# RG-LRU gates as four 64x64 products on quarters of the array, in a two-layer hybrid decoder trunk

## What is computed

```
def rglru_branch(xb, conv_w, conv_b, wa, ba, wx, bx, lam):
    xc = causal_dwconv(xb, conv_w) + conv_b
    xh = xc.reshape(Bsz, S, LRU_HEADS, LRU_HEAD_DIM)          # 8 heads of 64 channels
    r = sigmoid(einsum('bshi,hij->bshj', xh, wa) + ba)        # gate a
    ig = sigmoid(einsum('bshi,hij->bshj', xh, wx) + bx)       # gate x
    log_a = -LRU_C * r * softplus(-lam)
    a = exp(log_a);  mult = sqrt(-expm1(2.0 * log_a))
    h = scan(a, mult * ig * xc)
```

## Time and profile before

| | us |
|---|---|
| median of three runs (1820.25 to 1823.0) | 1821.43 |
| profiled execution, its time | 1824.21 |
| profiled execution, its span | 1822.4 |
| PE busy (share of the span) | 1668.1 (92%) |
| DVE busy | 1252.0 (69%) |
| ACT busy | 772.3 (42%) |
| POOL busy | 232.8 (13%) |
| mean DMA rate over the span | 206 GB/s |

### The profile page before, as it was taken

How to read it: one execution, slowest core, us unless ns; L and a number is a source line. 1 busy time by engine, 2 the same in 40 slices (tenths; PEclk the granted TensorE clock), 3 DMA queues, 4 the chain that set the end, 5 groups by cost and what they waited for, 6 DMA issues and landing times.

```text
span 1822.4 us, 23064 instructions
## 1 busy us (share of the span) xinstructions
PE 1668.1 (92%) x7527; PEld 1295.7 (71%) x7527; DVE 1252.0 (69%) x2361; ACT 772.3 (42%) x1014; POOL 232.8 (13%) x281
## 2 busy tenths in 40 slices
PE   2339999989999999999998999999999999999995
PEld 1237778767777877777886777777877777776884
DVE  5885984796598479666862587398468558743758
ACT  2135444554444454432126554554555464442220
POOL 2142111111111111100004111111111111100000
PEclk9559999999999999999998999999999999999998
DMA  7999888988987998867646888987888887755422
GB/s 261 379 330 255 199 209 212 234 218 200 232 209 205 215 234 208 209 199 273 206 142 180 196 192 193 216 191 192 205 196 202 189 204 186 178 163 200 146 93 104
DMA packets 322945, 376.07 MB, mean 206 GB/s; under 512 B 27064, under 2 KB 224032, under 8 KB 319784
## 3 DMA queue, kind: packets, MB, share of 16 engines
q1 hardware_dynamic: 294632, 272.36, 46.4%
q0 software_dynamic: 28224, 102.77, 31.3%
HBM read 261.81 MB, written 10.51 MB: 149 GB/s over the span
## 4 chain that ended last, share of the span: by engine, by line
PE 58%; DVE 29%; issue 6%; DMA 3%; ACT 2%; SPq 1%; DVEq 0%; POOL 0%; ACTq 0%; POOLq 0%
PE bank L1012 18%; PE bank L975 11%; PE bank L968 11%; PE bank L969 11%; DVE work L1330 9%; DVE ada_acc L1338 3%; DVE work L1338 3%; DMA w_lo<-raw 2%; DVE work L1192 2%; DVE work L1191 2%; DVE carry L1338 2%; PE bank L992 2%; DVE y_t L1338 1%; DVE work L1334 1%; DVE carry L1330 1%
## 5 line engine op out<-in xcount | busy, mean ns | idle before, releaser
L968 PE MATMUL bank<-op_hi,w_hi 128*128 128x512 f32 x1536 | 619.7, 403 | 0.0
L969 PE MATMUL bank<-op_lo,w_hi 128*128 128x512 f32 x1536 | 605.0, 394 | 0.0
L975 PE MATMUL bank<-op_hi,w_lo 128*128 128x512 f32 x1536 | 380.1, 390 | 6.3 <-DMA w_lo<-raw 6.3
L604 ACT ACTIVATE w_hi<-raw 128x1024 fp32r<-128x1024 f32 x196 | 207.8, 1060 | 405.8 <-PE bank L969 318.6
L968 PEld LDWEIGHTS bank<-op_hi,w_hi 128*128 128x128 f32 x1536 | 292.2, 190 | 89.1 <-issue 22.1
L975 PEld LDWEIGHTS bank<-op_hi,w_lo 128*128 128x128 f32 x1536 | 287.9, 188 | 68.4 <-DMA w_lo<-raw 8.9
L969 PEld LDWEIGHTS bank<-op_lo,w_hi 128*128 128x128 f32 x1536 | 292.1, 190 | 60.6 <-issue 1.9
L556 POOL DMA_DIRECT2D w_lo<-raw x196 | 170.4, 869 | 1085.5 <-ACT w_lo L607 1066.4
L607 ACT ACTIVATE w_lo<-raw 128x1024 fp32r<-128x1024 f32 x196 | 207.2, 1057 | 109.8 <-PE bank L975 109.7
L1338 DVE SCALAR_TENSOR_TENSOR ada_acc<-ada_in,cond,ada_acc 128x512 f32<-128x512 f32 (+1 forms) x234 | 181.5, 775 | 77.9 <-DMA ada_in<-in_w_ada 56.2
L742 ACT ACTIVATE w_hi<-raw 128x1024 fp32r<-128x1024 f32 x56 | 59.5, 1062 | 231.7 <-PE bank L1012 215.3
(11 more groups left out here) (227 smaller groups left out, 1587.6 us busy)
## 6 DMA issues: line engine op xcount, KB each, us to landing
w_lo<-raw POOLq DMA_DIRECT2D x196, 512.0 KB, 5.0
raw<-in_w_in SPq DMA_DIRECT2D x192, 512.0 KB, 4.3
ada_in<-in_w_ada SPq DMA_DIRECT2D x256, 256.0 KB, 4.2
raw<-in_w_out SPq DMA_DIRECT2D x64, 512.0 KB, 4.2
raw<-in_w_ada SPq DMA_DIRECT2D x27, 512.0 KB, 6.6
ada_in<-in_w_ada SPq DMA_DIRECT2D x18, 512.0 KB, 6.5
rot<-in_w_ada SPq DMA_DIRECT2D x10, 512.0 KB, 6.4
bias_t<-in_w_ada SPq DMA_DIRECT2D x9, 512.0 KB, 6.5
```

The lines of the kernel that those rows point to most:

```text
L604: act.activation(w_hi[:, n % NHL, :], raw[:, n % NRAW, :], ACT.Copy).then_inc(s.hi_done.sem, 1)
L968: pe.matmul(o, w_hi[:, n % NHL, w], op_hi[:, k, :], start=k == 0, stop=False)
L969: mm = pe.matmul(o, w_hi[:, n % NHL, w], op_lo[:, k, :], start=False, stop=False)
L975: mm = pe.matmul(o, w_lo[:, n % NHL, w], op_hi[:, k, :], start=False, stop=k == KT - 1)
```

## The change

Each gate's product of a head becomes a matmul of its own, 64 rows by 64 columns, so that four of them stand on the four quarters of the array. With h the head (the rows) and i the gate, the product goes to bank 5 + h, on partitions 64 * (h ^ i): gate a stays on its head's partitions, and gate x lands on the other half. The weights are dense, 64 columns wide, with no zeros and no memset, and a pass loads them with two transfers of 128 partitions (`mix_in` counts 64, not 96). ACT reads each quarter with a tanh of its own and writes gate x back to its head's partitions: four tanh of 64 partitions for two of 128. On PE both banks are waited for ahead of the first product, and a nop that isn't fused into the next instruction stands behind these waits. A bank's signal comes with its second product.

```diff
-        lru_w = sb("lru_w", [P, 2, P])
+        lru_w = sb("lru_w", [P, 2, 64])
...
-                        for h in range(2):
-                            at = step * P + 64 * h
-                            sp.dma_start(lru_w[64 * h:64 * h + 64, i, 64 * h:64 * h + 64], src[at:at + 64, :])\
-                                .then_inc(s.mix_in.sem, 16)
+                        sp.dma_start(lru_w[:, i, :], src[step * P:(step + 1) * P, :]).then_inc(s.mix_in.sem, 16)
...
-            pool.memset(lru_w[:, :, :], 0.0).then_inc(const_done.sem, 1)
...
-                        act.wait_ge(s.full[5].sem, s.full[5].at(1, ct))
-                        act.wait_ge(s.full[6].sem, s.full[6].at(1, ct))
-                        act.activation(lru_s[0], bank[5][:, :], ACT.Tanh, scale=0.5,
-                                       bias=lru_c[:, l, bass.ds(ct + 4, 1)]).then_inc(s.free[5].sem, 1)
-                        act.activation(lru_s[1], bank[6][:, :], ACT.Tanh, scale=0.5,
-                                       bias=lru_c[:, l, bass.ds(ct + 8, 1)]).then_inc(s.free[6].sem, 1)
-                        act.wait_ge(s.free[5].sem, s.free[5].at(1, ct))
+                        for h in range(2):
+                            act.wait_ge(s.full[5 + h].sem, s.full[5 + h].at(1, ct))
+                            to = slice(64 * h, 64 * h + 64)
+                            for i in range(2):
+                                at = 64 * (h ^ i)
+                                e = act.activation(lru_s[i][to, :], bank[5 + h][at:at + 64, :], ACT.Tanh, scale=0.5,
+                                                   bias=lru_c[to, l, bass.ds(ct + (4 + 4 * i), 1)])
+                            e.then_inc(s.free[5 + h].sem, 1)
+                        for h in range(2):
+                            act.wait_ge(s.free[5 + h].sem, s.free[5 + h].at(1, ct))
...
-                        pe.wait_ge(s.mix_in.sem, s.mix_in.at(96, ct))
+                        pe.wait_ge(s.mix_in.sem, s.mix_in.at(64, ct))
                         pe.wait_ge(s.p_copy.sem, s.p_copy.at(0, ct))
+                        for h in range(2):
+                            is_free(5 + h, 0)
+                        pe.nop(nofuse=True)
                         for i in range(2):
-                            is_free(5 + i, 0)
-                            fill(5 + i, pe.matmul(bank[5 + i][:, :], lru_w[:, i, :], xc, start=True, stop=True))
+                            for h in range(2):
+                                rows_, to = slice(64 * h, 64 * h + 64), 64 * (h ^ i)
+                                mm = pe.matmul(bank[5 + h][to:to + 64, :], lru_w[rows_, i, :], xc[rows_, :],
+                                               start=True, stop=True)
+                                if i:
+                                    fill(5 + h, mm)
```

More of the change, by code:

```diff
@@ L277, in trunk @@
             s.s5_in = signal("s5_in" + n, 64)
-            s.mix_in = signal("mix_in" + n, 96)
+            s.mix_in = signal("mix_in" + n, 64)
             s.scale_sum = signal("scale_sum" + n) if l < DEPTH - 1 else None
@@ L784, in turn @@
                 return pe.transpose(out_, in_, ident[0:n, 0:n]).then_inc(sig.sem, 1)
-            pe.wait_ge(const_done.sem, 14)
+            pe.wait_ge(const_done.sem, 13)
             pe.wait_ge(row_dma.sem, 16 * 15 * DEPTH)
@@ L1216, in score_max @@
                         if t == 0 and h == 0:
-                            dve.wait_ge(s.mix_in.sem, s.mix_in.at(96, ct))
+                            dve.wait_ge(s.mix_in.sem, s.mix_in.at(64, ct))
                         if t == ST - 1 and h == 1:
@@ L1346, in _ @@
             steps = Signal(setup_dve.sem, 0, 0)
-            dve.wait_ge(const_done.sem, 14)
+            dve.wait_ge(const_done.sem, 13)
             for s in layers:
```

## The result

| | before | changed |
|---|---|---|
| median, six runs each | 1821.79 us (1819.71 to 1824.33) | 1827.92 us (1825.30 to 1831.29) |
| ratio, 95% interval | | 1.0035 (1.002 to 1.005) |
| profiled execution, time and span | 1824.21, 1822.4 | 1830.15, 1828.0 |
| mean granted clock of it | 0.961 | 0.954 |

A forecast was written before the change was run, and what follows sets the result against it. No engine bounds the whole; in layer 1 the path runs gates, PE to fourth scores, DVE to normalised second head, PE. Layer 1 -1.8, loads -0.7, clock +0.2: -2.3 us, from 1821.43 to 1819.1, range 1816.6 to 1823.2.

The forecast's parts named there:

- forecast 1.33, perhaps 1.28: Gate products on PE: eight passes overlap and take the time of two, 1.33 us instead of 1.79, gain 0.46 per pass.
- that rival: Gates on PE: two weight loads per row group show at 0.13 us each, 0.5 us on top of 1.33; 1821.1 us; chance 0.08.
- forecast 4 x 0.46: Layer 1: the gates' 0.46 us goes through in each of four passes, 1.8 us in all.
- DVE's wait for the fourth scores: Sign in layer 1: DVE's wait before the fourth query block's scores falls from 1.23 to 0.8 us.
- The evictions: Four tanh of 64 partitions on ACT instead of two of 128: about 1.2 us more work, covered, worth 0.
- ACT's next wait: Sign on ACT: its wait of 2.72 us takes up the evictions' 0.7 us delay and becomes 2.0.
- the low part of piece 9: Weight piece split on ACT behind the gates, moved by POOL DMA: 0.7 of 2.2 us slack used, PE not waiting.
- The loads: Two SP transfers instead of four, first pass of layer 0: gain 0.7 us, ends 0 and 1.29.
- The clock term: Layer 0, PE's longer wait before the third drive product: new clock falls add 0.2 us, ends 0 and 3.5.
- in layer 0 the gain is worth 0: Layer 0 gates: the saved 0.46 us only lengthens PE's wait before the third drive product, 1.46 to 1.9 us.

The follow-up runs named there:

- the shortened kernel: The kernel before, with the two gate products of layer 0 cut to 368 of 512 columns: ratio 1.0032 to the kernel before, median 1826.92 us.
- the padded one: The changed kernel plus one unread fp32 matmul of 256 columns behind the gates in layer 0: ratio 0.9993 to the kernel before, median 1821.61 us.

## Why the prediction was wrong

**The mechanisms of the instructions were right.** Quarters overlap all four: 1.28 us for the gates, forecast 1.33, perhaps 1.28. The Trainium skill ("TensorE: Matmul & The Clock Gate", Why this matters for your kernels) has row and column packing combine; this trace agrees, with eight passes in 1.09 us. The rule of the Trainium skill (same page, Part 3, what overlaps and what doesn't) that only a different row group hides a weight load would have put two loads of each row group in the open, twice. This trace differs: all eight loads, of 131 ns each, stand within 0.21 us from 1196.44, while the first four passes run, so that rival is out as well. Layer 1 gained 4 x 0.51 us, forecast 4 x 0.46. DVE's wait for the fourth scores did not shrink to 0.8 us, as I had written: it waits for the third scores too (0.61 us before), and the gain went in there; nothing hung on it.

**The evictions** cost more than I said, and nothing all the same. The four tanh last 2.78 us, and from the first to the second tanh of `lru_s[0]` it is 2.93 us against 1.15 of old: 1.8 us more, not 1.2. The timeline of ACT, and DVE's first use:

```profile
1198.95 2.78 ACT L662 ACTIVATE work<-bank,lru_c 64x512 f32<-64x512 f32 x4
1201.88 0.82 ACT L667 ACTIVATE work<-work,lru_c 128x512 f32<-128x512 f32 x1
...
1208.15 1.06 ACT L600 ACTIVATE w_hi<-raw 128x1024 fp32r<-128x1024 f32 x1 [1.13 <-PE bank L975]
...
1208.17 0.42 DVE L1340 TENSOR_SCALAR work<-work 128x512 f32<-128x512 f32 x1
```

ACT's next wait is 1.13 us, not 2.0, and DVE still comes 3.5 us after the square root. For the low part of piece 9 I counted the POOL issue of 0.86 us twice: the 4.6 us to landing begin with the issue, so the slack was 3.1 us, not 2.2. PE doesn't wait for it.

**The loads**, 0.7 us by my sum, are worth nothing that the times show, and at most a few tenths by the profiles. What failed here is that I saw only the queue ahead of the raw load of piece 3 and not its own wait for a free place.

**The clock term is the step that failed.** I had its row, one of its two places and its direction, and put it at +0.2 us with ends 0 and 3.5; even the upper end was too small. Three things were wrong in it. I took a fall to last 3.4 us as in that row; with the longer wait more than half of them last twice as long, and a long one costs the pass 2.2 us where a short one costs 0.65. I left their number open, where the wait's growth from 1.5 to 2 us raised it from 3 in 8 passes to 18 in 20. And I priced the falls at the drive alone, while the dearer ones stand at the transposes. Between the two profiles the term measures some 8 us in place of 0.2 (3.8 at the drive and 4.5 at the transposes). Over all runs the longer wait costs 6 us by the shortened kernel (1.0032) and 6 to 8 by the padded one (0.9993 against 1.0026 and 1.0035). Why the falls at the transposes became more, at a wait there that stayed the same, is open, and that they did is read from few profiles; that those there cost the changed kernel much is shown by filling that wait alone (9 us). Behind the term stands a sentence that I wrote as if it closed the matter: in layer 0 the gain is worth 0, because PE's wait of 1.46 us covers it. A cover that grows was counted as free.

## What to carry to other kernels

When TensorE's work shrinks ahead of a place where it waits anyway, don't count the saving as zero: it becomes idle time, and here a wait of 1.5 us that became 2 us cost 6 us in clock, three times what the change saved. In the trace of the kernel before, look in the windows behind each wait of PE for stretches at 0.50, and price both their number and their length, and separately where they are followed by slack and where by PE's own limit. Products that nobody reads, put into such a wait and short enough to end within it, made the changed kernel 0.3 to 0.4% faster than the kernel before, and the kernel before 0.2% faster: more than the change itself could give (2 us, 0.11%).

## What the runs showed of the hardware that I had not expected

Falls of the granted clock at waits as short as 1.5 us, in 3 of 8 passes, and a clock that stays at 0.50 for 6.8 us while PE is busy through all of it (365.1 to 371.9). Four quarters of the array run four fp32 passes in the time of one: 1.09 us for eight, where two row groups take 1.13 for four. And four tanh of 64 partitions out of a bank take 0.7 us each, as long as one of 128 partitions did before (0.69), and more than the 0.59 us of the copies of 64 partitions.
